# Two products of the feed-forward layers in one 512-column matmul, with the small terms summed apart

## The chip, the cores and the metric

The kernel runs on one core of a Trainium2 chip. The metric is the device time of one execution in microseconds (us), the median of the runs; lower is better. Engines are named as the profile names them: PE is the matmul engine, PEld its weight loads, ACT the scalar engine, DVE the vector engine, POOL the third elementwise engine, SP the engine that issues the weight transfers. Each engine works through its own instructions in the order in which they are written, and they signal each other with semaphores.

## The reference

Four layers at 256 tokens and width 1024, one batch, all in 32-bit floats: stick-breaking attention, retention, gated linear attention and a sparse attention, each followed by a feed-forward layer. The parts that the change touches, cut to their core:

```
def squared_relu_mlp(h, w_up, w_down):      # layers 1 and 2, hidden width 4096
    u = jax.nn.relu(h @ w_up)
    return (u * u) @ w_down

def conv_ffn(h, w_up, conv_w, conv_b, w_down):   # layers 3 and 4, hidden width 2816
    u = h @ w_up                                  # 2 x 2816 columns
    up = jnp.pad(u, ((0, 0), (CONV_WIDTH - 1, 0), (0, 0)))
    u = conv_b + up[:, 0:S] * conv_w[0]
    for j in range(1, CONV_WIDTH):                # CONV_WIDTH = 3
        u = u + up[:, j:j + S] * conv_w[j]
    gate, val = jnp.split(u, 2, axis=-1)
    return (jax.nn.silu(gate) * val) @ w_down

def rmsnorm(x, g):
    y = x * lax.rsqrt(jnp.mean(x * x, axis=-1, keepdims=True) + EPS)
    return y * g
```

## The kernel before, in words

**Products.** Every operand of a large product is split into a high part, rounded to the matmul's `fp32r` type, and a low part, the rest (`w_hi`, `w_lo`, `x_hi`, `x_lo`, `y_hi`, `y_lo`). A product is three matmuls into one PSUM region: high times high, high times low, low times high (`mm3`, lines 562 to 564).

**Weights.** They come in 212 pieces of 128 x 2048 floats, in the order of use. SP loads half pieces into `ring`, which holds four halves; half `q` may be loaded when DVE is done with half `q` - 4 (`stream`, line 373). ACT rounds a half into `w_hi` (line 1222), DVE subtracts and writes `w_lo` (line 1689). `w_hi` and `w_lo` hold four pieces: `refill(g)` loads piece `g` + 4 when PE is done with piece `g`. PE waits for `w_lo` in `split`.

**A feed-forward layer** is `hidden` on PE, and `mlp` (layers 1 and 2) or `ffn` (layers 3 and 4) on ACT and DVE. An up unit `u` is one weight piece, 256 hidden columns in two groups `j` of 128 and eight steps `k` over the width: 48 matmuls of 256 columns that fill one PSUM bank (`transposed`, or `first_unit` for unit 0). MLP layers have 16 up units, conv layers 22. The elementwise engines turn a unit into `y_hi` and `y_lo`. A down piece multiplies them into the accumulators in banks 0 to 3 (`accumulate`, 24 matmuls of 512 columns, `close` for the last ones). In an MLP layer each two up units are followed by two down pieces, one pair of units late. In a conv layer (`ffn`) eight up units come first, then one down piece after each two up units, three pairs late; the last two down pieces are done in `close`, behind all others. Units use six banks in turn (0 and 1 for the first two, then 4 to 7), and unit `u` from 6 on waits until unit `u` - 4 is read out (`freed`).

**The elementwise work of a conv unit**, in the order of each engine:

- DVE: read the bank and multiply by the tokens' scale (`scaled`, line 1736); product of the unit before (1827); `w_lo` of the piece that fell due one step earlier (`refill_behind`, 1689 twice); `y_lo` of the unit before (1833); the two taps of the convolution (1850 twice, 1855 twice).
- ACT: base of the convolution (1308 twice), `y_hi` of the unit before (1302), `w_hi` of the next piece (1222 twice), then silu (1315), which waits for the taps.

An MLP unit has relu (1276) and square into `y_hi` (1279) on ACT, the square (1792) and `y_lo` (1796) on DVE, and one refill on each.

**The tokens' scale.** The norm's factor is applied behind the matmul. POOL computes it from the sum of squares, `spread` on PE turns it into a row (line 553), ACT copies that out of PSUM. In a conv layer PE does `spread` between unit 0 and unit 1.

**The start.** `sb_first` makes the first two pieces in eight quarters; `turn_over` transposes the input in four parts, which ACT and DVE turn into `x_hi` and `x_lo`; `x_tiles` waits for them. `sb_z_` is the attention's first score product and waits for the scaled queries and keys (`sb_unit` on DVE).

## Time and profile before

| | before |
|---|---|
| median of 3 runs | 1383.16 us (1382.28 to 1383.33) |
| the profiled execution's own time | 1384.69 us |
| its span, first to last instruction | 1383.0 us |
| instructions in it | 23122 |
| PE busy | 1345.8 us, 97% |
| DVE busy | 907.9 us, 66% |
| ACT busy | 724.5 us, 52% |
| mean granted PE clock | 0.994 |

The span and the median measure the same thing to 0.2 us; the profiled execution took 1.7 us around its span. Matmuls overlap each other, so a matmul's duration is longer than the distance to the next one; times of a stream of matmuls are read from the distance of their starts.

### The profile page before, as it was taken

How to read it: one execution, taken by the hardware profiler on the slowest of the kernel's cores; microseconds unless marked ns; L12 is line 12 of the kernel's file. 1: busy time of each engine (PE TensorE's matmuls, PEld its weight loads, DVE VectorE, ACT ScalarE, POOL GpSimd, SP SyncE). 2: the span in 40 equal slices, each digit the busy share in tenths (PEclk: the TensorE clock that was granted, in tenths of full speed). 3: DMA queues.
4: the chain of work that ended last, by engine and by line, in shares of the span. 5: the costliest groups of instructions: out<-in, count | busy, mean ns of one | idle time of the engine just before them, and what ended most of it. 6: DMA issues, size and time to landing. Idle time of an engine off the chain costs nothing.

```text
span 1383.0 us, 23122 instructions
## 1 busy us (share of the span) xinstructions
PE 1345.8 (97%) x8826; PEld 1206.3 (87%) x8826; DVE 907.9 (66%) x1417; ACT 724.5 (52%) x1155; POOL 119.2 (9%) x123
## 2 busy tenths in 40 slices
PE   8999999999999999999999999999999988999998
PEld 7887999989987889999888789999888866899997
DVE  4756655557645656555568558777768755697775
ACT  5555544445334545444464446555577535565553
POOL 0001000002500000000002300000002332000000
PEclk9999999999999999999999999999999999999999
DMA  6535655555553446565543345555654310355551
GB/s 229 181 126 196 227 179 201 181 187 172 193 184 126 164 154 227 180 200 183 184 168 125 120 154 183 183 183 187 200 192 153 123 62 32 121 190 187 187 191 70
DMA packets 63887, 231.09 MB, mean 167 GB/s; under 512 B 7088, under 2 KB 7344, under 8 KB 63792
## 3 DMA queue, kind: packets, MB, share of 16 engines
q1 hardware_dynamic: 62208, 224.42, 48.7%
q10 hardware_dynamic: 1584, 5.31, 1.1%
q8 instruction: 70, 1.15, 0.3%
q14 instruction: 25, 0.20, 0.1%
HBM read 228.66 MB, written 1.05 MB: 166 GB/s over the span
## 4 chain that ended last, share of the span: by engine, by line
PE 88%; DVE 5%; ACT 3%; issue 2%; DMA 1%; POOL 0%; POOLq 0%; SPq 0%; DVEq 0%; ACTq 0%
PE ps L562 27%; PE ps L563 26%; PE ps L564 26%; DVE w_lo L1689 2%; DMA ring<-ws 1%; ACT w_hi L1222 1%; DVE x_lo L1709 1%; PE ps L932 1%; ACT x_hi L1242 1%; PE ps L534 1%; PE ps L1124 1%; PE ps L1104 1%; PE ps L856 0%; ACT arena L1217 0%; DVE arena L2242 0%
## 5 line engine op out<-in xcount | busy, mean ns | idle before, releaser
L1689 DVE TENSOR_TENSOR w_lo<-ring,w_hi 128x1024 fp32r<-128x1024 f32 x424 | 513.3, 1250 | 174.4 <-ACT w_hi L1222 173.9
L1222 ACT ACTIVATE w_hi<-ring 128x1024 fp32r<-128x1024 f32 x424 | 429.2, 1052 | 238.9 <-PE ps L564 189.2
L562 PE MATMUL ps<-x_hi,w_hi 128*128 128x256 f32 x1600 | 455.0, 284 | 0.5 <-DVE x_lo L1709 0.5
L563 PE MATMUL ps<-x_lo,w_hi 128*128 128x256 f32 x1600 | 452.7, 283 | 0.0
L564 PE MATMUL ps<-x_hi,w_lo 128*128 128x256 f32 x1600 | 452.6, 283 | 0.0
L562 PEld LDWEIGHTS ps<-x_hi,w_hi 128*128 128x128 f32 x1600 | 306.7, 192 | 4.0 <-issue 3.0
L563 PEld LDWEIGHTS ps<-x_lo,w_hi 128*128 128x128 f32 x1600 | 306.8, 192 | 1.0
L564 PEld LDWEIGHTS ps<-x_hi,w_lo 128*128 128x128 f32 x1600 | 306.8, 192 | 0.0
L562 PE MATMUL ps<-w_hi,y_hi 128*128 128x512 f32 x560 | 221.0, 395 | 2.3 <-issue 2.3
L563 PE MATMUL ps<-w_lo,y_hi 128*128 128x512 f32 x560 | 219.0, 391 | 0.0
L564 PE MATMUL ps<-w_hi,y_lo 128*128 128x512 f32 x560 | 218.6, 390 | 0.0
L562 PEld LDWEIGHTS ps<-w_hi,y_hi 128*128 128x128 f32 x560 | 105.6, 189 | 23.9 <-issue 3.4
L564 PEld LDWEIGHTS ps<-w_hi,y_lo 128*128 128x128 f32 x560 | 105.6, 189 | 22.5
L562 PE MATMUL ps<-w_hi,x_hi 128*128 128x512 f32 (+1 forms) x304 | 121.2, 399 | 3.9 <-DVE x_lo L1709 1.8
L563 PEld LDWEIGHTS ps<-w_lo,y_hi 128*128 128x128 f32 x560 | 105.8, 189 | 20.1
L564 PE MATMUL ps<-w_hi,x_lo 128*128 128x512 f32 (+1 forms) x304 | 115.4, 380 | 0.0
L563 PE MATMUL ps<-w_lo,x_hi 128*128 128x512 f32 (+1 forms) x304 | 115.0, 378 | 0.0
L1736 DVE SCALAR_TENSOR_TENSOR arena<-ps,arena 128x512 f32<-128x512 f32 x64 | 44.1, 690 | 69.0 <-PE ps L564 68.6
L408 POOL TENSOR_TENSOR stat<-stat,power 128x1 f32<-128x1 f32 x20 | 11.6, 585 | 885.4 <-DVE stat L1684 702.7
L1308 ACT ACTIVATE arena<-arena,sm 128x256 f32<-128x256 f32 x88 | 48.2, 595 | 56.7 <-DVE arena L1736 56.7
L562 PEld LDWEIGHTS ps<-w_hi,x_hi 128*128 128x128 f32 x304 | 57.1, 188 | 19.1 <-issue 4.2
L1242 ACT ACTIVATE x_hi<-ps,sm 128x128 fp32r<-128x128 f32 x128 | 35.5, 377 | 70.8 <-PE ps L534 70.8
(227 smaller groups left out, 1305.4 us busy)
## 6 DMA issues: line engine op xcount, KB each, us to landing
ring<-ws SPq DMA_DIRECT2D x424, 512.0 KB, 4.8
tab<-tables ACTq DMA_DIRECT2D x3, 550.0 KB, 5.4
rowg<-rows ACTq DMA_DIRECT2D x3, 512.0 KB, 6.1
h<-x SPq DMA_DIRECT2D x4, 256.0 KB, 5.9
out<-arena SPq DMA_DIRECT2D x4, 256.0 KB, 2.2
arena<-decay ACTq DMA_DIRECT2D x1, 768.0 KB, 8.7
sm<-small ACTq DMA_DIRECT2D x1, 642.0 KB, 4.3
arena<-narrow ACTq DMA_DIRECT2D x1, 296.0 KB, 3.1
```

The lines of the kernel that those rows point to most:

```text
L534: r = nc.tensor.transpose(ps[:, base + k // 2, t * T + (k % 2) * P:t * T + (k % 2 + 1) * P], h[:, t, k * P:(k + 1) * P], ident)
L562: mm(o, lh, rh, start=start, stop=False, skip_group_check=True)
L563: mm(o, lh, rl, start=False, stop=False, skip_group_check=True)
L564: return mm(o, ll, rh, start=False, stop=stop, skip_group_check=True)
L932: r = mm(o, keys, q, start=True, stop=True, skip_group_check=True)
L1104: r = nc.tensor.transpose(ps[:, 6 + i, j * P:(j + 1) * P], ns_s[it % 3][:, i, j * P:(j + 1) * P], ident)
L1124: r = mm(o, v[:, 0, :], p_[:, t * P:(t + 1) * P], start=False, stop=False, skip_group_check=True)
L1222: A(w_hi[:, q // 2 % RING, c:c + HALF], ring[:, q % RAW, :], ACT.Copy).then_inc(hi_ready, 1)
L1242: r = A(dst[:, k, t * P:(t + 1) * P], ps[:, base + b, t * T + (k % 2) * P:t * T + (k % 2 + 1) * P], ACT.Copy, scale=gain(n, k))
L1308: r = A(conv[:, u % 2, e, :], conv_in[:, u % 2, e, :], ACT.Identity, scale=par(u, 4 + e), bias=par(u, 6 + e))
L1689: V.tensor_tensor(w_lo[:, g % RING, v], ring[:, q % RAW, :], w_hi[:, g % RING, v].bitcast(F32), ALU.subtract).then_inc(lo_ready, 1)
L1736: return V.scalar_tensor_tensor(dst, src.rearrange("p (a t) -> p a t", t=T), by, sc.unsqueeze(1).broadcast_to([P, 2, T]), ALU.mult, ALU.mult)
```

## The change

`x_hi` and `x_lo` become the two halves of one tensor `x_both`, side by side for each step `k`. In the up units of all four feed-forward layers `wide` takes the place of `transposed` and `first_unit`: for each `k` and `j` one matmul of 512 columns multiplies `w_hi` by both parts of x, the high product into columns 0 to 255 of a bank, the low one into columns 256 to 511, and one matmul of 256 columns adds `w_lo` times `x_hi` to the latter. A unit is then 16 matmuls of 512 and 16 of 256 columns and fills two banks (`pair_bank`): 0 and 1, 2 and 3, and then 4 and 5 in turn with 6 and 7. Unit `u` from 4 on waits until unit `u` - 2 is read out.

The two sums are added on the way out. ACT copies the small one of the unit to SBUF, DVE adds the large one from PSUM (now `freed`). In the MLP layers DVE then makes the squared relu in one instruction and ACT copies it into `y_hi`. In the conv layers DVE multiplies by the scale in a second instruction. `spread` of the conv layers moves from behind unit 0 to the middle of unit 1, into bank 6, and the first one of the kernel to the middle of piece 3. The first block's quarters, transposes and the elementwise work beside them are reordered.

```diff
-            def first_unit(g, b, n):
+            def wide(g, b, first=None, mid=None):
...
+                for part, j in [(e, j) for e in range(2) for j in range(2)] if first is not None else [(None, 0), (None, 1)]:
+                    if j == 1 and mid is not None:
+                        mid()
+                    for k in range(KT) if part is None else (lower, upper)[part]:
+                        if j == 0 and k % 4 == 0:
+                            split(g, k // 4)
+                        if j == 0 and first is not None:
+                            x_tiles(first, k)
+                        c = k * 256 + j * P
+                        mm(ps[:, b + j, :], w_hi[:, s, c:c + P], x_both[:, k, :, :], start=k == 0, stop=False,
+                           skip_group_check=True)
+                        r = mm(ps[:, b + j, T:2 * T], w_lo[:, s, c:c + P], x_hi[:, k, :], start=False, stop=k == KT - 1,
+                               skip_group_check=True)
+                    if (part, j) == (0, 0):
+                        turn_over(first, 1, part=upper)
...
                 def up(c):
                     for u in (2 * c, 2 * c + 1):
-                        if u >= 6:
-                            pe.wait_ge(freed, at + u - 3)
-                        if u == 0:
-                            first_unit(st.up(c), bank(u), n)
-                        else:
-                            transposed(st.up(c) + u % 2, bank(u))
-                        if u == 0 and n in SCALE_OF:
-                            spread(n)
+                        if u >= 4:
+                            pe.wait_ge(freed, at + u - 1)
+                        if u == 3 and n in SCALE_OF:
+                            pe.wait_ge(scale_ready, SCALE_OF[n] + 1)
+                        wide(st.up(c) + u % 2, pair_bank(u), first=n if u == 0 else None,
+                             mid=(lambda: spread(n, 6)) if u == 1 and n in SCALE_OF else None)
...
-                for q in range(2):
-                    split(g, q)
-                    quarter(0, q)
+                split(g, 0)
+                quarter(0, 0)
                 turn_over(0, 1, part=lower)
+                split(g, 1)
+                quarter(0, 1)
                 turn_over(0, 0, part=upper)
                 quarter(1, 0)
                 quarter(1, 1).then_inc(done, 1)
+                turn_over(0, 1, part=upper)
                 split(g + 1, 0)
                 quarter(0, 2)
-                turn_over(0, 1, part=upper)
                 quarter(1, 2)
...
             sb_first(G_SB, (0, 1))
-            spread(0, 4)
             transposed(G_SB + 2, 2)
-            transposed(G_SB + 3, 3)
+            transposed(G_SB + 3, 3, mid=lambda: spread(0, 4))
```

ACT in an MLP unit:

```diff
-                            act.wait_ge(ready, u - 1)
-                        A(relu[:, u % 2, :], ps[:, bank(u), :], ACT.Relu).then_inc(freed, 1)
-                        act.wait_ge(freed, u + 1)
+                            act.wait_ge(sq, at + u - 1)
+                        A(relu[:, u % 2, :].rearrange("p (a t) -> p a t", t=T), ps[:, b:b + 2, T:2 * T], ACT.Copy)\
+                            .then_inc(low, 1)
+                        act.wait_ge(sq, at + u + 1)
                         i = st.tiles(c)[2 * (u % 2)]
-                        A(y_hi[:, i:i + 2, :], relu[:, u % 2, :].rearrange("p (a t) -> p a t", t=T), ACT.Square)\
+                        A(y_hi[:, i:i + 2, :], square[:, u % 2, :].rearrange("p (a t) -> p a t", t=T), ACT.Copy)\
                             .then_inc(hh, 1)
```

ACT in a conv unit:

```diff
-                        act.wait_ge(freed, at + u + 1)
+                        act.wait_ge(done, st.up(c) + u % 2 + 1)
+                        if u >= 2:
+                            act.wait_ge(freed, at + u - 1)
+                        b = pair_bank(u)
+                        A(conv_small[:, u % 2, :, :], ps[:, b:b + 2, T:2 * T], ACT.Copy).then_inc(low, 1)
+                        act.wait_ge(scaled_in, at + u + 1)
```

DVE in an MLP unit:

```diff
-                        dve.wait_ge(freed, u + 1)
-                        v = relu[:, u % 2, :]
-                        V.tensor_tensor(square[:, u % 2, :], v, v, ALU.mult).then_inc(sq, 1)
+                        dve.wait_ge(low, at + u + 1)
+                        v, b = relu[:, u % 2, :], pair_bank(u)
+                        o = v.rearrange("p (a t) -> p a t", t=T)
+                        V.tensor_tensor(o, ps[:, b:b + 2, 0:T], o, ALU.add).then_inc(freed, 1)
+                        dve.wait_ge(freed, at + u + 1)
+                        V.scalar_tensor_tensor(square[:, u % 2, :], v, 0.0, v, ALU.max, ALU.mult).then_inc(sq, 1)
```

DVE in a conv unit:

```diff
-                        dve.wait_ge(done, g + 1)
-                        scaled(conv_in[:, u % 2, :, :], ps[:, bank(u), :], scale).then_inc(freed, 1)
+                        dve.wait_ge(low, at + u + 1)
+                        b, v = pair_bank(u), conv_in[:, u % 2, :, :]
+                        V.tensor_tensor(v, ps[:, b:b + 2, 0:T], conv_small[:, u % 2, :, :], ALU.add).then_inc(freed, 1)
+                        dve.wait_ge(freed, at + u + 1)
+                        V.tensor_tensor(v, v, scale.unsqueeze(1).broadcast_to([P, 2, T]), ALU.mult).then_inc(scaled_in, 1)
```

ACT, then DVE, in the first block:

```diff
+            hi(2)
             sumsq(0)
-            hi(2)
...
+            lo(2)
             fold(0)
-            lo(2)
...
             dve.wait_ge(scale_ready, SCALE_OF[0] + 1)
+            sb_unit(0)
             refill(G_SB + 1)
-            sb_unit(0)
+            sb_unit(1)
             refill(G_SB + 2)
-            sb_unit(1)
```

How the instructions stand on ACT in a conv layer, from one silu to the next, before the change (`arena` holds all working tiles, so that silu is `arena<-arena` 128x256; behind each row stand the semaphores that it waits for):

```order
L1315 ACTIVATE arena<-arena 128x256 [waits ffn_conv]
L1308 ACTIVATE arena<-arena,sm 128x256 [waits ffn_freed]
L1308 ACTIVATE arena<-arena,sm 128x256
L1302 ACTIVATE y_hi<-arena 128x256 [waits ffn_product]
L1222 ACTIVATE w_hi<-ring 128x1024 [waits weights_in2,piece_done]
L1222 ACTIVATE w_hi<-ring 128x1024 [waits weights_in3]
L1315 ACTIVATE arena<-arena 128x256 [waits ffn_conv]
```

The same place with the change:

```order
L1331 ACTIVATE arena<-arena 128x256 [waits ffn_conv]
L1321 ACTIVATE arena<-ps 128x512 [waits ffn_freed,piece_done]
L1324 ACTIVATE arena<-arena,sm 128x256 [waits ffn_scaled]
L1324 ACTIVATE arena<-arena,sm 128x256
L1313 ACTIVATE y_hi<-arena 128x256 [waits ffn_product]
L1231 ACTIVATE w_hi<-ring 128x1024 [waits weights_in0,piece_done]
L1231 ACTIVATE w_hi<-ring 128x1024 [waits weights_in1]
L1331 ACTIVATE arena<-arena 128x256 [waits ffn_conv]
```

The copy of the small sum of a unit (L1321) stands behind the silu of the unit before it.

DVE in a conv layer, one unit before the change, up to the read-out of the next:

```order
L1736 SCALAR_TENSOR_TENSOR arena<-ps,arena 128x512 [waits piece_done]
L1827 TENSOR_TENSOR arena<-arena 128x256 [waits ffn_silu]
L1689 TENSOR_TENSOR w_lo<-ring,w_hi 128x1024 [waits piece_hi] x2
L1833 TENSOR_TENSOR y_lo<-arena,y_hi 128x256 [waits ffn_hi,ffn_product]
L1850 SCALAR_TENSOR_TENSOR arena<-arena,sm 128x255 [waits ffn_base,ffn_freed]
L1850 SCALAR_TENSOR_TENSOR arena<-arena,sm 128x255
L1855 SCALAR_TENSOR_TENSOR arena<-arena,sm 128x254 [waits ffn_tap]
L1855 SCALAR_TENSOR_TENSOR arena<-arena,sm 128x254
L1736 SCALAR_TENSOR_TENSOR arena<-ps,arena 128x512 [waits piece_done]
```

And with the change:

```order
L1861 TENSOR_TENSOR arena<-ps,arena 128x512 [waits ffn_small]
L1863 TENSOR_TENSOR arena<-arena 128x512 [waits ffn_freed]
L1847 TENSOR_TENSOR arena<-arena 128x256 [waits ffn_silu]
L1705 TENSOR_TENSOR w_lo<-ring,w_hi 128x1024 [waits piece_hi] x2
L1853 TENSOR_TENSOR y_lo<-arena,y_hi 128x256 [waits ffn_hi,ffn_product]
L1873 SCALAR_TENSOR_TENSOR arena<-arena,sm 128x255 [waits ffn_base,ffn_scaled]
L1873 SCALAR_TENSOR_TENSOR arena<-arena,sm 128x255
L1878 SCALAR_TENSOR_TENSOR arena<-arena,sm 128x254 [waits ffn_tap]
L1878 SCALAR_TENSOR_TENSOR arena<-arena,sm 128x254
L1861 TENSOR_TENSOR arena<-ps,arena 128x512 [waits ffn_small]
```

One instruction for the read-out has become two, and the first of them no longer waits for PE's `piece_done` but for ACT's copy (`ffn_small`).

## Rows read from the trace of the kernel before

**Rows 1.** The page: the chain that ended last, by engine.
```profile
PE 88%; DVE 5%; ACT 3%; issue 2%; DMA 1%; POOL 0%; POOLq 0%; SPq 0%; DVEq 0%; ACTq 0%
```

**Rows 2.** Windows of a conv layer: stretch, length, busy time of each engine, clock, DMA.
```profile
860.00:1000.00 140.00, 140.00 (x966) 130.97 (x965) 107.74 (x169) 78.64 (x116) 0.00 (x0) 1.00 0.56 188
```

**Rows 3.** Timeline of PE, end of a conv layer: start, duration, what.
```profile
1002.03 0.39 PE L564 MATMUL ps<-w_hi,y_lo 128*128 128x512 f32 x1
...
1004.07 0.39 PE L564 MATMUL ps<-w_hi,y_lo 128*128 128x512 f32 x1
1004.30 1.03 PE L534 MATMUL ps<-sm,h 128*128 128x128 f32 x8
```

**Rows 4.** Timeline of DVE, start of the first conv layer.
```profile
829.52 0.68 DVE L1736 SCALAR_TENSOR_TENSOR arena<-ps,arena 128x512 f32<-128x512 f32 x1
...
839.13 0.69 DVE L1736 SCALAR_TENSOR_TENSOR arena<-ps,arena 128x512 f32<-128x512 f32 x1 [0.43 <-PE ps L564]
839.74 0.42 DVE L1827 TENSOR_TENSOR arena<-arena 128x256 f32<-128x256 f32 x1
840.07 2.35 DVE L1689 TENSOR_TENSOR w_lo<-ring,w_hi 128x1024 fp32r<-128x1024 f32 x2
842.34 0.42 DVE L1833 TENSOR_TENSOR y_lo<-arena,y_hi 128x256 fp32r<-128x256 f32 x1
842.67 0.87 DVE L1850 SCALAR_TENSOR_TENSOR arena<-arena,sm 128x255 f32<-128x255 f32 x2
843.58 0.88 DVE L1855 SCALAR_TENSOR_TENSOR arena<-arena,sm 128x254 f32<-128x254 f32 x2
844.89 0.69 DVE L1736 SCALAR_TENSOR_TENSOR arena<-ps,arena 128x512 f32<-128x512 f32 x1 [0.43 <-PE ps L564]
```

**Rows 5.** Timeline of ACT beside it.
```profile
840.86 0.40 ACT L1302 ACTIVATE y_hi<-arena 128x256 fp32r<-128x256 f32 x1
841.16 1.99 ACT L1222 ACTIVATE w_hi<-ring 128x1024 fp32r<-128x1024 f32 x2
844.49 0.42 ACT L1315 ACTIVATE arena<-arena 128x256 f32<-128x256 f32 x1 [1.34 <-DVE arena L1855]
```

**Rows 6.** Groups of ACT by form: busy us, mean ns, idle before.
```profile
L1276 ACT ACTIVATE arena<-ps 128x512 f32<-128x512 f32 x32 | 19.1, 597 | 83.2 <-PE ps L564 83.2
```

**Rows 7.** Timeline of DVE around a down piece.
```profile
902.83 2.36 DVE L1689 TENSOR_TENSOR w_lo<-ring,w_hi 128x1024 fp32r<-128x1024 f32 x2
```

**Rows 8.** Timeline of ACT around the same down piece.
```profile
907.96 1.06 ACT L1222 ACTIVATE w_hi<-ring 128x1024 fp32r<-128x1024 f32 x1 [0.29 <-DMA ring<-ws]
910.35 1.06 ACT L1222 ACTIVATE w_hi<-ring 128x1024 fp32r<-128x1024 f32 x1 [1.33 <-DMA ring<-ws]
```

**Rows 9.** The page: DMA issues, KB each, median us from issue to landing.
```profile
ring<-ws SPq DMA_DIRECT2D x424, 512.0 KB, 4.8
```

**Rows 10.** Timeline of DVE, end of the first conv layer.
```profile
993.58 0.42 DVE L1833 TENSOR_TENSOR y_lo<-arena,y_hi 128x256 fp32r<-128x256 f32 x1 [0.56 <-ACT y_hi L1302]
...
1003.13 1.29 DVE L1763 TENSOR_TENSOR h<-ps,h 128x512 f32<-128x512 f32 x2
```

**Rows 11.** Waits: total us, times, longest us.
```profile
PE ps L553 <- POOL stat L408: 2.9, 2, 1.5
```

**Rows 12.** Timeline of PE in the third mixer, behind a wait.
```profile
793.12 0.47 PE L562 MATMUL ps<-w_hi,y_hi 128*128 128x512 f32 x1 [2.34 <-issue]
```

**Rows 13.** Windows around it.
```profile
788.00:800.00 12.00, 9.66 (x40) 7.71 (x39) 7.16 (x10) 4.62 (x7) 2.50 (x2) 0.86 0.53 174
```

**Rows 14.** Timeline of PE, first block and first score product.
```profile
13.92 0.50 PE L562 MATMUL ps<-w_hi,x_hi 128*128 128x512 f32 x1 [0.71 <-DVE x_lo L1709]
...
20.29 0.50 PE L562 MATMUL ps<-w_hi,x_hi 128*128 128x512 f32 x1 [1.14 <-DVE x_lo L1709]
...
39.77 0.28 PE L564 MATMUL ps<-x_hi,w_lo 128*128 128x256 f32 x1
41.23 0.50 PE L758 MATMUL ps<-arena 64*128 64x128 f32 x4 [1.18 <-DVE arena L1736]
```

49 lines of the change are left out of this document (22 added, 27 removed).

## The prediction

> **What bounds the kernel now.** I read the chain that ended last first. It is 88% PE [rows 1]; in a conv layer PE is busy in every one of 140 us, while DVE works in 107.7 and ACT in 78.6 of them [rows 2]. By these averages any saving of matmul time counts, and DVE has a quarter of its time to spare. The average misleads, though: within a conv layer there are stretches of up units alone, and there the timeline of DVE shows only 0.43 us of idle time in a unit of 5.76 us (839.13 to 844.89) [rows 4]. That is the number on which this prediction turns. The reader should see a loop over two engines [rows 4, 5]: DVE reads out a unit, makes the product of the unit before, two halves of `w_lo`, `y_lo` and the taps; ACT's silu waits for the taps (844.49, 1.34 idle [rows 5]).
>
> **Matmuls.** A unit is now 48 matmuls of 256 columns in 5.76 us, 0.120 us each [rows 4]. Nine intervals of 512-column matmuls take 1004.07 - 1002.03 = 2.04 us, 0.227 each [rows 3]. So three small ones, 0.360, become 0.227 + 0.120 = 0.347, and a unit takes 16 x 0.347 = 5.55 us: 0.21 less. The mixed sequence is not in the trace. It could cost nothing beyond its parts, or at worst lose the 0.013 us again and save nothing; I take the parts, since the engine already passes from one width to the other at every down piece. The Trainium skill, "TensorE: Matmul & The Clock Gate", section "Back-to-back issue gap", gives 2.5 ns beyond the columns for a matmul alone; the rows show some 13 ns for both widths [rows 3, 4]. By the skill's figure a unit would save 0.04 us instead of 0.21, and the two MLP layers 1.3 instead of the 6.8 below; the measurement decides.
>
> **MLP layers.** 32 units x 0.21 = 6.8 us less, if the elementwise work keeps up. DVE's loop is add 0.72 (0.69 and 0.03 to the next instruction that needs it), squared relu 0.72, wait for ACT's copy 0.60 + 0.03 [rows 6], `y_lo` 0.61, `w_lo` 2.27 and some 0.4 until its `w_hi` is there: 5.3 us, under 5.55. ACT's next copy doesn't wait for anything late on DVE, and after each two units come two down pieces, 2 x 24 x 0.227 = 10.9 us, with refills alone. The four units at the start could lose a few tenths; I take none. Banks: unit u needs what u - 2 left, a whole unit of 5.55 us ago, and the read-out takes 1.4 us. **-6.8 us** (0 to -6.8).
>
> **Conv layers, unit by unit.** The new order puts ACT's copy of the small sum behind the silu of the unit before, and DVE's add behind that copy. From one add to the next [rows 4 to 6]: add to multiply 0.72; multiply to product 0.61; product to `w_lo` 0.33; two halves 2.27; `y_lo` 0.33; first taps to second 0.91; second taps 0.88; silu starts 0.03 later and lets the next ACT instruction start 0.33 after its own start (as the 0.30 behind `y_hi`); copy 0.60; 0.03 to DVE. Sum 7.04 us, of which the new copy, its place behind silu, and the second pass are 1.71. PE offers a unit each 5.55 us, so it isn't PE that sets the pace any more but this loop. The bank pairs allow PE two units ahead; from unit 5 on it waits for `freed`, 7.04 - 5.55 = 1.5 us each time.
>
> The Trainium skill, "PSUM — Partial Sum Buffer", section "Engine vs sequencer instructions", calls the ScalarE and VectorE queues strict FIFO. If ACT could take the copy ahead of silu, the loop would be only the 6.05 us up to the end of the taps; by the rule it is 7.04. No row of before shows the case, since nothing that stood behind a silu was ready ahead of it.
>
> **Conv layers, with a down piece.** Behind every second unit ACT also fills `w_hi` for the piece of the down step, and stands in front of the next copy until its second half has landed. SP can issue that half only when DVE has made `w_lo` of the second half it replaces. That `w_hi` starts 910.35 - 902.83 = 7.52 us behind DVE's start on the pair, having waited 1.33 for the transfer [rows 7, 8]. The pair starts 0.72 + 0.61 + 0.33 = 1.66 behind the add, so the half starts at 9.18; 0.94 later (1.99 less 1.05, rows 5) the copy, 0.63 later the next add: 10.75. By the median landing of 4.8 [rows 9] from 1.66 + 2.36 it is 4.02 + 4.8 + 0.03 + 0.94 + 0.63 = 10.4. I take 10.6. A pair of units and its down piece then take 7.04 + 10.6 = 17.6 us against PE's 2 x 5.55 + 5.44 = 16.55 (now 16.96). The loop binds here too.
>
> **Sum of a conv layer.** DVE's first read-out is at 829.52 [rows 4] behind `w_lo` work that doesn't change. To the next one 5.35 (no product or refill yet: 0.72 + 0.69 + ACT's base 1.1 + 0.91 + 0.88 and the 1.0 of silu and copy), six loops 42.2, seven pairs 7 x 17.64 = 123.5: the last add is at 1000.6. Its `y_lo` is ready 6.05 + silu 0.45 + product 0.45 + `y_hi` 0.43 + 0.45 = 7.83 later, and only then does `close` start, at 1008.4. Now it starts 30 matmuls ahead of the transposes: 1004.30 - 6.8 = 997.5 [rows 3]. **+10.9 us** in each of the two layers, all savings of matmuls and waits inside it already swallowed.
>
> Behind the first conv layer there is more. From `y_lo` at 994.0 to the residual at 1003.13 DVE needs 9.1 us of refills [rows 10], paced by transfers. Starting at 1008.4 it reaches the residual at 1017.5 and has both halves at 1018.7; PE comes to its transposes at 1008.4 + 6.8 = 1015.2. **+3.5 us.** The last layer has no such refills.
>
> **Clock.** PE's wait ahead of `close` becomes long: unit 21 ends with its two down pieces about 6 us before. After an idle 2.34 us [rows 12] the granted clock over 12 us was 0.86 of 2.4 GHz, the rest at the 1.2 GHz level [rows 13]: 0.14 x 12 = 1.7 us lost. In the first conv layer that hides in the wait for the residual; in the last it counts: **+1.7** (0 to +4). Waits of 1.5 us, as after the spread [rows 11], are not expected to cost it.
>
> **Spread of the scale.** PE now idles 1.46 us at each of the two [rows 11]. Moving it half a unit back removes this, but the first read-out is at 829.52 either way: nothing.
>
> **First block.** PE waits 0.71 and 1.14 us for `x_lo` [rows 14]; each transpose now stands one quarter (6 x 0.227 = 1.4 us) earlier, which covers both, with 0.15 each to refill the pipe. `sumsq` behind `hi(2)` and the spread within piece 3 cost nothing, since a full piece of 5.76 us covers them; the statistics come 2 us later and so does `sb_v`, with two pieces in between. `sb_unit(1)` no longer stands behind a refill, so the 1.18 at the score product [rows 14] goes. Sum 0.71 + 1.14 + 1.18 + 0.15 x 3 = 3.5, a half more for later transfers that start earlier: **-4.0** (-2 to -4.5).
>
> **Sum.** -6.8 - 4.0 + 2 x 10.9 + 3.5 + 1.7 = +16.2. The profiled execution had a span of 1383.0 and 1.7 around it; its span becomes 1399.2. The median of the runs, 1383.16, is the 1.5 us lower of the two totals and becomes 1399.4; I say 1399.5.
>
> **Rivals.**
>
> - *The loop holds, but the transfer is not waited for* (ends on the other side). If the second half landed 1.7 us sooner, the copy would follow at 6.05 + 0.36 + 1.88 + 0.63 = 8.9 and a pair take 15.96, less than PE's 16.55. PE then catches up in the pairs what it lost in the six loops, and `close` starts as now: 1383.2 - 6.8 - 4.0 = 1372. It decides at 10.6 - 16.2 / 14 = 9.4 us for the step with a down piece. For it: landing times scatter. Against: the same transfer behind the same pair of `w_lo` already makes ACT wait 1.33 us [rows 8], with less work on its way. 12%.
> - *The elementwise work never binds*: all 76 units save 0.21 (16.0), the two spreads 2 x 1.6, the start 4.0: 1360. For it: DVE's busy share of 77% [rows 2]. Against: 0.43 us of slack [rows 4], and 1.71 added. 5%.
> - *As forecast, but transfers land later in the new rhythm*, 0.7 us each of 14: 1409. 4%.
> - *A matmul costs 2.5 ns beyond its columns*, so that the MLP layers gain 1.3: 1405. The skill's figure named above; the intervals speak against it [rows 3, 4]. 2%.
> - *The changes cancel*: within 0.2% of now, if the step with a down piece is near 9.4. 3%.
>
> The forecast has the remaining 74%. Its own range is 1391 to 1407: ends of the MLP term (7 us up), of the start (2 up), 10.4 and 10.75 in the step with a down piece (3 down, 2 up), the clock (2 down, 2 up), and half of the tail. 0.2% is 2.8 us, about what a measurement of this kernel can tell from no change. Faster 12 + 5 = 17%, same 3%, slower 80%. The range for 8 in 10 is 1388 to 1408.
>
> **What the profile will show.** Right: the 512-column matmul on x starts 0.120 behind the small one, and that one 0.227 behind it; in MLP layers no idle PE; in conv layers PE idle about 1.5 us ahead of units 5 to 7 for DVE's add, 0.5 to 1 ahead of every odd unit later for `w_lo`, and about 6 us ahead of `close` for `y_lo`; adds 7.0 us apart, 10.6 with a down piece. Wrong: adds 5.55 us apart in the first eight units, which would mean that ACT's copy doesn't wait for silu; no DMA wait of ACT behind odd units; a clock below 1 in the up units. The forecast breaks most easily at the 10.6.

## The result, and the profile with the change

| | before, same chip | with the change |
|---|---|---|
| median of 4 runs | 1382.89 us | 1407.96 us (1403.55 to 1411.57) |
| profiled execution: own time, span | | 1403.55 us, 1401.8 us |
| instructions | | 20860 |
| mean granted PE clock | | 0.991 |

The ratio is 1.018, 95% interval 1.0149 to 1.0211: 25 us slower. The spans of the two profiled executions differ by 1401.8 - 1383.0 = 18.8 us. The profiled execution is the fastest of the four; what follows explains its 18.8 us, and the spread of the others is taken up at the end.

The chain that ended last, by engine, answers [rows 1]:

```profile
PE 63%; DVE 19%; DMA 6%; issue 5%; ACT 5%; POOL 1%; SPq 0%; DVEq 0%; POOLq 0%; ACTq 0%
```

PE has lost a quarter of the chain, and transfers have 6% of it. Busy shares hardly show this: over the same 140 us as in [rows 2], DVE is busy in 113.2 instead of 107.7 us, ACT in 82.9 instead of 78.6, and PE in 130.9 instead of all 140. The second row is the stretch around `close`:

```profile
860.00:1000.00 140.00, 130.90 (x674) 109.97 (x672) 113.22 (x178) 82.90 (x128) 0.00 (x0) 0.99 0.54 177
996.00:1008.00 12.00, 7.10 (x24) 5.76 (x25) 9.01 (x13) 5.65 (x7) 0.00 (x0) 0.72 0.59 180
```

DVE in the ramp, as the first eight up units of a conv layer are called from here on, answering [rows 4]:

```profile
840.95 0.69 DVE L1861 TENSOR_TENSOR arena<-ps,arena 128x512 f32<-128x512 f32 x1 [0.97 <-ACT arena L1321]
841.67 0.69 DVE L1863 TENSOR_TENSOR arena<-arena 128x512 f32<-128x512 f32 x1
842.28 0.42 DVE L1847 TENSOR_TENSOR arena<-arena 128x256 f32<-128x256 f32 x1
842.62 2.35 DVE L1705 TENSOR_TENSOR w_lo<-ring,w_hi 128x1024 fp32r<-128x1024 f32 x2
844.89 0.42 DVE L1853 TENSOR_TENSOR y_lo<-arena,y_hi 128x256 fp32r<-128x256 f32 x1
845.22 0.87 DVE L1873 SCALAR_TENSOR_TENSOR arena<-arena,sm 128x255 f32<-128x255 f32 x2
846.13 0.88 DVE L1878 SCALAR_TENSOR_TENSOR arena<-arena,sm 128x254 f32<-128x254 f32 x2
847.98 0.69 DVE L1861 TENSOR_TENSOR arena<-ps,arena 128x512 f32<-128x512 f32 x1 [0.97 <-ACT arena L1321]
```

and ACT beside it:

```profile
843.71 1.99 ACT L1231 ACTIVATE w_hi<-ring 128x1024 fp32r<-128x1024 f32 x2
847.04 0.42 ACT L1331 ACTIVATE arena<-arena 128x256 f32<-128x256 f32 x1 [1.34 <-DVE arena L1878]
847.36 0.58 ACT L1321 ACTIVATE arena<-ps 128x512 f32<-128x512 f32 x1
```

Two engines wait for each other in a ring: DVE's add waits 0.97 us for ACT's copy, the copy stands behind silu, and silu has waited 1.34 us for DVE's taps. One round is 847.98 - 840.95 = 7.03 us.

ACT where a down piece comes in:

```profile
892.28 0.42 ACT L1331 ACTIVATE arena<-arena 128x256 f32<-128x256 f32 x1 [1.34 <-DVE arena L1878]
893.26 1.06 ACT L1231 ACTIVATE w_hi<-ring 128x1024 fp32r<-128x1024 f32 x1 [0.56 <-DMA ring<-ws]
895.89 1.06 ACT L1231 ACTIVATE w_hi<-ring 128x1024 fp32r<-128x1024 f32 x1 [1.57 <-DMA ring<-ws]
896.86 0.58 ACT L1321 ACTIVATE arena<-ps 128x512 f32<-128x512 f32 x1
```

and DVE's adds ahead of it and behind it:

```profile
886.18 0.69 DVE L1861 TENSOR_TENSOR arena<-ps,arena 128x512 f32<-128x512 f32 x1 [0.97 <-ACT arena L1321]
...
897.47 0.69 DVE L1861 TENSOR_TENSOR arena<-ps,arena 128x512 f32<-128x512 f32 x1 [2.96 <-ACT arena L1321]
```

The copy, which needs nothing but PE's sum, stands behind two transfers, and the add follows 11.29 us after the last one. PE pays in four places (timeline of PE, one row for each kind of wait): for the bank that DVE's add frees, for `w_lo`, ahead of `close`, and at the transposes behind it:

```profile
848.72 0.50 PE L603 MATMUL ps<-x_both,w_hi 128*128 128x512 f32 x1 [1.11 <-DVE arena L1861]
...
907.53 0.47 PE L603 MATMUL ps<-x_both,w_hi 128*128 128x512 f32 x1 [1.24 <-DVE w_lo L1705]
...
1000.90 0.80 PE L569 MATMUL ps<-w_hi,y_hi 128*128 128x512 f32 x1 [6.24 <-DVE y_lo L1853]
1011.54 1.25 PE L541 MATMUL ps<-sm,h 128*128 128x128 f32 x8 [2.02 <-DVE h L1779]
```

In the MLP layers PE has no such waits; the edge of a down piece and a unit shows both widths:

```profile
228.82 0.39 PE L571 MATMUL ps<-w_hi,y_lo 128*128 128x512 f32 x1
229.05 0.39 PE L603 MATMUL ps<-x_both,w_hi 128*128 128x512 f32 x1
...
230.10 0.40 PE L603 MATMUL ps<-x_both,w_hi 128*128 128x512 f32 x1
230.34 0.28 PE L605 MATMUL ps<-x_both,w_lo 128*128 128x256 f32 x1
230.45 0.40 PE L603 MATMUL ps<-x_both,w_hi 128*128 128x512 f32 x1
```

A good way to place a difference is to cut the span at marks that every version has. Here they are PE's first transposes of each norm, which begin the start, the layers and the mixers in turn (us; each entry is the distance of two marks read from PE's timeline; the last two columns are explained below):

| stretch | before | change | difference | `copy_ahead_all` | `copy_ahead_of_refill` |
|---|---|---|---|---|---|
| start and first mixer | 129.1 | 124.7 | -4.4 | 125.9 | 125.6 |
| MLP layer 1 | 179.7 | 177.9 | -1.8 | 178.2 | 177.9 |
| second mixer | 198.5 | 198.4 | -0.1 | 198.5 | 198.4 |
| MLP layer 2 | 181.5 | 179.7 | -1.8 | 179.7 | 180.1 |
| third mixer | 124.7 | 124.7 | 0.0 | 124.7 | 123.1 |
| conv layer 1 | 190.8 | 206.1 | +15.3 | 189.0 | 194.4 |
| fourth mixer | 177.4 | 175.4 | -2.0 | 176.0 | 176.2 |
| conv layer 2 to the end | 201.3 | 214.9 | +13.6 | 197.4 | 203.3 |
| span | 1383.0 | 1401.8 | +18.8 | 1369.4 | 1379.0 |

### The profile page after: what moved, and what is told of

The parts are those of the page before. It is cut to its first block, busy times and chain, and to the rows that moved or that the text cites. A ratio compares the mean times of both kernels' runs of the same rounds, so it can differ in the third digit from the quotient of the medians.

```text
span 1401.8 us, 20860 instructions
## 1 busy us (share of the span) xinstructions
PE 1342.4 (96%) x7610; PEld 1141.0 (81%) x7610; DVE 961.3 (69%) x1493; ACT 746.8 (53%) x1199; POOL 120.1 (9%) x123
## 4 chain that ended last, share of the span: by engine, by line
PE 63%; DVE 19%; DMA 6%; issue 5%; ACT 5%; POOL 1%; SPq 0%; DVEq 0%; POOLq 0%; ACTq 0%
PE ps L569 14%; PE ps L571 13%; PE ps L570 13%; PE ps L603 10%; DVE w_lo L1705 7%; DMA ring<-ws 6%; PE ps L605 5%; DVE arena L1861 2%; DVE arena L1863 2%; DVE arena L1878 2%; ACT arena L1321 2%; DVE arena L1873 2%; ACT w_hi L1231 1%; DVE arena L1847 1%; PE ps L941 1%
## 5 line engine op out<-in xcount | busy, mean ns | idle before, releaser
L603 PE MATMUL ps<-x_both,w_hi 128*128 128x512 f32 x1216 | 432.7, 399 | 15.0 <-DVE arena L1861 8.2
L605 PE MATMUL ps<-x_both,w_lo 128*128 128x256 f32 x1216 | 340.6, 280 | 0.0
L603 PEld LDWEIGHTS ps<-x_both,w_hi 128*128 128x128 f32 x1216 | 228.3, 188 | 76.5 <-issue 11.0
L605 PEld LDWEIGHTS ps<-x_both,w_lo 128*128 128x128 f32 x1216 | 229.5, 189 | 0.9
L569 PE MATMUL ps<-w_hi,x_both 128*128 128x512 f32 (+1 forms) x304 | 121.9, 401 | 1.7 <-DVE x_both L2285 0.9
L571 PE MATMUL ps<-w_hi,x_both 128*128 128x512 f32 (+1 forms) x304 | 116.1, 382 | 0.0
L570 PE MATMUL ps<-w_lo,x_both 128*128 128x512 f32 (+1 forms) x304 | 115.8, 381 | 0.0
L569 PE MATMUL ps<-x_both,w_hi 128*128 128x256 f32 x384 | 110.1, 287 | 0.0
L570 PE MATMUL ps<-x_both,w_hi 128*128 128x256 f32 x384 | 108.6, 283 | 0.0
L571 PE MATMUL ps<-x_both,w_lo 128*128 128x256 f32 x384 | 108.6, 283 | 0.0
L415 POOL TENSOR_TENSOR stat<-stat,power 128x1 f32<-128x1 f32 x20 | 11.6, 586 | 909.3 <-DVE stat L1700 712.9
L569 PEld LDWEIGHTS ps<-x_both,w_hi 128*128 128x128 f32 x384 | 73.5, 191 | 1.4 <-issue 1.3
L570 PEld LDWEIGHTS ps<-x_both,w_hi 128*128 128x128 f32 x384 | 73.6, 192 | 0.0
```

Source lines behind the costliest of these rows:

```text
L569: mm(o, lh, rh, start=start, stop=False, skip_group_check=True)
L570: mm(o, lh, rl, start=False, stop=False, skip_group_check=True)
L571: return mm(o, ll, rh, start=False, stop=stop, skip_group_check=True)
L603: mm(ps[:, b + j, :], w_hi[:, s, c:c + P], x_both[:, k, :, :], start=k == 0, stop=False, skip_group_check=True)
L605: r = mm(ps[:, b + j, T:2 * T], w_lo[:, s, c:c + P], x_hi[:, k, :], start=False, stop=k == KT - 1, skip_group_check=True)
```

## The experiments

The theory was the prediction's: the ring of ACT's copy, silu and the taps, and the transfers ahead of the copy. Its rival was that the change costs time elsewhere too, in the matmuls or by new transfers. All kernels are versions of the changed one, except where the text says that it is one of the kernel before. Ratios are to the kernel before on the same chip, where its median was 1384.4 to 1386.5 us; each is given with its 95% interval. The expectations went by the 1382.9 us of the first chip. A time "brought to it" below is the ratio times 1382.9, and it is the one to hold against an expected time.

### ACT's copy moved ahead of silu

`small(u)` is the wait and copy of the small sum of unit `u`, which in the change begins a unit. `copy_ahead_part` moves it ahead of silu, but not past the refill of a down piece:

```diff
-                        act.wait_ge(done, st.up(c) + u % 2 + 1)
...
-                        A(conv_small[:, u % 2, :, :], ps[:, b:b + 2, T:2 * T], ACT.Copy).then_inc(low, 1)
+                        if u == 0:
+                            small(0)
...
                         refill(st.up(c) + u % 2)
+                        if u % 2 == 0 or c < st.ahead:
+                            small(u + 1)
                         act.wait_ge(conv_done, at + u + 1)
...
                         refill(st.down(c))
+                    if c + st.ahead + 1 < st.chunks:
+                        small(2 * (c + st.ahead + 1))
```

> ACT copies the small sum of conv unit u+1 before the silu of unit u, wherever no down piece stands between them; the work itself and the bank pairs stay as changed. Theory (the loop over two engines sets the pace, because the copy stands behind silu): DVE's adds come 5.96 us apart in the first eight units instead of 7.03 (taps 0.79 to the next add instead of 1.86), a step with a down piece stays near 10.6, a pair takes about 16.7 and is bound by PE; PE waits for DVE fall to about 0.3 us a unit, the wait ahead of the last down pieces shrinks from 6 us to about 1, and the total is 1364 to 1372 us. Rival (what costs is the added DVE and ACT work, or two bank pairs instead of six banks, in whatever order): the total stays within 4 us of the changed kernel's 1408.

Measured: 1380.9 us, ratio 0.9963 (0.9947 to 0.9979). Adds are 5.97 us apart in the ramp, and 10.0 to 11.3 us with a down piece, much as without the edit. Brought to the first chip that is 1377.8 us, 6 above the expected range. A pair with its down piece still takes 10.8 + 5.97, about 16.8 us, no less than PE's own 16.8, so DVE never catches up with PE, and PE waits 2.07 and 2.97 us ahead of the two `close`.

`copy_ahead_all` also puts the copy between silu and the down piece's refill:

```diff
                     if u == units - 1:
                         product_hi(u)
+                    elif c >= st.ahead:
+                        small(u + 1)
```

> As the run with the copy ahead of silu, but the copy also stands ahead of the refill that follows a down piece, so that it doesn't wait for that refill's transfer. Theory: steps with a down piece fall to PE's pace (about 11.1 us with the pair's other step at 5.6), PE never waits for w_lo in the conv layers, no long wait ahead of the last down pieces; 1362 to 1368 us, at or some us below the partial version. Rival (added work or bank pairs): still above 1395 us. If transfers do not matter at all, it equals the partial version within 1 us.

Measured: 1370.73 us, ratio 0.9898 (0.9881 to 0.9914), 1% faster than before. DVE's adds in the ramp:

```profile
840.11 0.68 DVE L1869 TENSOR_TENSOR arena<-ps,arena 128x512 f32<-128x512 f32 x1
...
846.08 0.68 DVE L1869 TENSOR_TENSOR arena<-ps,arena 128x512 f32<-128x512 f32 x1
```

and ACT between them:

```profile
842.86 1.99 ACT L1231 ACTIVATE w_hi<-ring 128x1024 fp32r<-128x1024 f32 x2
844.76 0.58 ACT L1320 ACTIVATE arena<-ps 128x512 f32<-128x512 f32 x1
846.19 0.42 ACT L1337 ACTIVATE arena<-arena 128x256 f32<-128x256 f32 x1 [0.86 <-DVE arena L1886]
```

The copy now lies in the time in which ACT waited for the taps, and the add no longer waits. Steps with a down piece are 8.25 us, until the adds settle at 10.82 and 5.98 in turn, which is PE's own pair of 16.8. Everything the change lost in the conv layers comes from the place of one instruction. Brought to the first chip the time is 1368.8 us, 1 us above the expected range; the matmul pair gains less than was thought, as comes up below.

`copy_ahead_of_refill` makes the second move without the first: behind silu, but ahead of the down piece's refill.

```diff
+                        if u == 0 or u % 2 == 1 or c <= st.ahead:
+                            small(u)
...
                     if u == units - 1:
                         product_hi(u)
+                    elif c >= st.ahead:
+                        small(u + 1)
```

> The changed kernel with one edit: where a down piece makes VectorE and ScalarE do more in a step, ScalarE's copy of the next even unit stands behind silu as in the change, but ahead of the refill's split instead of behind it. In the first units of a convolution layer, which have no down piece, nothing is moved. Theory (the add waits for the copy, and the copy stands behind whatever ScalarE does after the gate): adds stay 7.03 us apart without a down piece; a step with one falls from 10.6 us to about 8.2 (5.97 of the short step plus 2.3 of the split), so that a pair of units takes about 15.3 us, less than the 16.7 that TensorE needs for its matmuls, and TensorE sets the pace again behind the ramp: 1371 to 1377 us. Rival (the 7.03 us loop of the first units costs most of it): above 1395 us.

Measured: 1382.2 us, ratio 0.9977 (0.9966 to 0.9988). The first step with a down piece, 868.75 to 877.00, and the step behind it:

```profile
868.75 0.69 DVE L1867 TENSOR_TENSOR arena<-ps,arena 128x512 f32<-128x512 f32 x1 [0.97 <-ACT arena L1320]
...
877.00 0.68 DVE L1867 TENSOR_TENSOR arena<-ps,arena 128x512 f32<-128x512 f32 x1
...
884.41 0.69 DVE L1867 TENSOR_TENSOR arena<-ps,arena 128x512 f32<-128x512 f32 x1 [1.36 <-ACT arena L1320]
```

Steps are 7.03 in the ramp and 8.25 with a down piece, as expected, and at the end 9.76 and 7.03 in turn at PE's pace; but brought to the first chip the total is 1379.7 us, 3 above the range. I had left out that the ramp's loss is not won back: the two conv layers take 5.4 and 5.9 us more than with both moves (table). So the place behind the refill costs 11.7 + 11.6 us of the change's loss, and the place behind silu the other 5.4 + 5.9. The moves don't add up in the other order (`copy_ahead_part` alone gains 13.0 + 14.1): whichever is made first gains most, since PE's pace limits both together.

### Half of each transfer left out

To tell the transfers from ACT's own work, each weight transfer behind the first four halves carries only half its columns; the rest of the weights in SBUF stays old, so that part of the product is made from other data. It is done to both kernels:

```diff
-                sp.dma_start(ring[:, q % RAW, :], src).then_inc(weights_in[q % RAW], 16)
+                n = HALF if turn is None and q < RAW else HALF // 2
+                sp.dma_start(ring[:, q % RAW, 0:n], src[:, 0:n]).then_inc(weights_in[q % RAW], 16)
```

> The changed kernel with each half weight piece transferred only half (512 of its 1024 columns; the other columns keep what the first four halves brought), so that a transfer lands sooner and the output is not the reference's. All instructions of the engines stay. Theory (the step with a down piece waits for the transfer of the refill, then the copy): adds without a down piece stay 7.03 us apart, steps with one fall from 10.6 us on average to about 9.2, PE regains in the pairs what it lost; 1388 to 1396 us. Rival (transfers are hidden, the work alone sets the pace): equal to the changed kernel's 1404 to 1411 us.

> The same halved transfers in the kernel before, as a control. Theory: PE is the bound there and transfers are hidden but for the start and some mixers; at most 3 us less than 1382.9. If halving the transfers made every kernel faster by more, the run of the changed kernel would tell nothing of its loop.

Measured: 1380.26 us for the change (0.9958, 0.9944 to 0.9972) and 1382.09 us for the kernel before (0.9972, 0.9961 to 0.9984). ACT at a down piece:

```profile
908.65 0.42 ACT L1332 ACTIVATE arena<-arena 128x256 f32<-128x256 f32 x1 [1.34 <-DVE arena L1879]
908.97 2.24 ACT L1232 ACTIVATE w_hi<-ring 128x1024 fp32r<-128x1024 f32 x2
911.11 0.58 ACT L1322 ACTIVATE arena<-ps 128x512 f32<-128x512 f32 x1
```

The split no longer waits, and the step falls from 10.6 to 9.2 us on the mean of both layers; the ramp keeps its 7.03. I had expected the changed kernel at least 11 us above this (1377.1 us, brought to the first chip). With a pair of 16.2, under PE's 16.8, DVE catches up with PE by half a microsecond in each pair, and the long waits ahead of `close` go (6.24 to 1.15 us in the first layer, 6.26 to nothing of note in the second). The two conv layers take 194.6 and 203.4 us, 11.5 less each than in the changed kernel. Seven steps with 1.4 us less waiting for transfers make 9.8 of each 11.5. In the control nothing of this is seen: its four feed-forward layers take 179.7, 181.6, 190.8 and 201.3 us, the kernel before's own times to 0.1. Its total fell by 3.9 us by the ratio, 0.9 more than the expected most; in the profiles the start gives 2.1 us and the third mixer 1.6.

### The feed-forward layers 3 and 4 as before

`conv_as_before` keeps the change in the MLP layers and at the start, and gives the conv layers their old matmuls, read-out and place of `spread`:

```diff
+                        if n in SCALE_OF:
...
+                            if u == 0:
+                                first_unit(st.up(c), bank(u), n)
+                            else:
+                                transposed(st.up(c) + u % 2, bank(u))
+                            if u == 0:
+                                spread(n)
+                            continue
```

`conv_as_before_spread` has `spread` in the middle of unit 1 instead.

> The MLP layers and the first block as changed; the two conv layers and their spread of the scale as before. Theory: all of the loss is in the conv layers, so this is faster than before: start 4.3 us and MLP layers 1.85 us each as the changed kernel's profile shows, 1374 to 1375 us; up to 2 us less if the third stretch of gain, in the sparse attention, is a matter of the layout and not of when it starts. Rival (part of the loss comes from the MLP layers' extra work, from the layout x_both or from transfers in general): above 1379 us.

> As the run with the conv layers as before, but their spread of the scale stands in the middle of unit 1. Theory: PE no longer idles 1.46 us at each of the two spreads and the pipe isn't refilled there, 1.6 us each: 3.2 us less than with the spread behind unit 0, so 1371 to 1372 us. Rival (DVE's first read-out is late either way, so nothing is gained): equal within 0.5 us.

Measured: 1376.65 us (0.9945, 0.9923 to 0.9967) and 1374.42 us (0.9918, 0.9901 to 0.9934); brought to the first chip 1375.3 and 1371.6, within 0.3 us of what was expected. The parts of the change outside the conv layers gain: 7.6 us by the first ratio, 9.3 by the spans.

The profile of the first has the two waits of 1.47 us at `spread` that [rows 11] show, the second has none of them. The medians differ by 2.2 us and their intervals overlap; the spans, 1373.7 and 1372.6, differ by 1.1. The marks of the table tell more. The conv layers take 191.3 and 201.3 us in the first and 189.8 and 199.6 in the second, 3.2 less together, as expected. The three traces with the old matmuls and the old place of `spread` (`before`, `half_transfers_before`, `conv_as_before`) have no less than 190.8 and 201.3, and `grouped_matmuls`, built on the second, has 189.2 and 199.6. What hides it in the spans is the clock in the third mixer: 123.0 us at a granted clock of 1.00 in the first, 124.6 at 0.99 in the second. Both have the same wait of PE of 2.3 us there, after which the clock fell in one execution and not in the other. All fourteen traces are of one kind or the other, 123.0 or 123.1 us in four and 124.6 or 124.7 in ten.

### The start as before

`start_as_before` is `copy_ahead_all` with the first block in its old order:

```diff
-                split(g, 0)
-                quarter(0, 0)
+                for q in range(2):
+                    split(g, q)
+                    quarter(0, q)
                 turn_over(0, 1, part=lower)
-                split(g, 1)
-                quarter(0, 1)
...
+            spread(0, 4)
             transposed(G_SB + 2, 2)
-            transposed(G_SB + 3, 3, mid=lambda: spread(0, 4))
+            transposed(G_SB + 3, 3)
...
```

> The kernel with the copy ahead everywhere, and the first block's order of quarters, transposes, halves, spread and scaled units as in the kernel before. Theory (the new order removes waits of 0.71, 1.14 and 1.18 us and the pipe's refill behind them): 4.0 to 4.4 us slower than with the new order. Rival (the gain of the start is given back later, at the waits for transfers and attention weights in the first mixer): equal within 1 us.

Measured: 1374.83 us (0.9924, 0.9909 to 0.994), against 1370.73 with the new order. PE's waits are back as in [rows 14]:

```profile
13.53 0.50 PE L569 MATMUL ps<-w_hi,x_both 128*128 128x512 f32 x1 [0.70 <-DVE x_both L1733]
19.88 0.50 PE L569 MATMUL ps<-w_hi,x_both 128*128 128x512 f32 x1 [1.14 <-DVE x_both L1733]
21.95 0.50 PE L569 MATMUL ps<-w_hi,x_both 128*128 128x512 f32 x1 [0.40 <-DVE w_lo L1713]
41.26 0.50 PE L767 MATMUL ps<-arena 64*128 64x128 f32 x4 [1.63 <-DVE arena L1760]
```

The first stretch of the table becomes 128.9 us, 3.0 more than `copy_ahead_all`'s, and no later stretch gives back more than 0.4 of it; the spans differ by 2.4 us and the medians by 4.1. So the gain of the start is real, 2.4 to 4.1 us by these figures, where 4.0 to 4.4 were expected.

### Why the matmul pair gains little

Over a whole layer the 512-column matmul of an up unit is followed after 235 ns (median over the kernel; 233 to 236 in single layers), where one of a down piece is followed after 227; the small one after 117 ns instead of 120. The pair takes 0.352 us and not 0.347, and a unit 5.63 us. Four kernels look for the reason. `grouped_matmuls` (on `conv_as_before_spread`) and `copy_ahead_grouped` (on `copy_ahead_all`) put four of one width behind each other:

```diff
+                        for k in ks:
+                            c = k * 256 + j * P
+                            r = mm(ps[:, b + j, T:2 * T], w_lo[:, s, c:c + P], x_hi[:, k, :], start=False,
+                                   stop=k == KT - 1, skip_group_check=True)
```

> The kernel with conv layers as before and the spread in unit 1, in which the MLP layers' up units issue four matmuls of 512 columns and then four of 256 instead of taking turns. Theory (a matmul of 256 columns between two of 512 costs some 5 ns a pair more than its two kinds cost in streams of their own: 235 + 117 against 227 + 120): pair 0.347, each MLP layer 16 x 16 x 5 ns = 1.3 us shorter, 2.6 in all. Rival (the extra is that of a matmul on x_both in two banks or of the pair's addresses, whatever the order): equal within 0.5 us.

> The copy ahead everywhere, with the matmuls grouped by four in the up units of all feed-forward layers. If grouping saves 5 ns a pair as supposed, 76 units x 16 x 5 ns = 6 us less than with the copy ahead alone, as far as DVE's 5.96 us a unit in the first eight conv units allows; if the order of the widths is indifferent, the same within 1 us.

Measured: 1374.46 us (0.9908, 0.9888 to 0.9929) and 1367.7 us (0.9866, 0.9849 to 0.9882). The order is not indifferent, but grouping by four gives less than half of what was hoped. Over all up units in which PE neither waited nor had the low clock, the mean pair is 0.350 us in both grouped kernels and 0.352 or 0.353 in every other one. The MLP layers take 177.4 and 179.2 to 179.3 us, where all ten other traces with the new matmuls have 177.8 to 178.2 and 179.7 to 180.1; in `copy_ahead_grouped` the four feed-forward layers together take 2.6 us less than in `copy_ahead_all`. The ratios go the same way (0.9866 against 0.9898, intervals that just touch). The two spans, 1369.1 and 1369.4 us, don't show it, because the profiled execution of `copy_ahead_grouped` was the slowest of its four, at a granted clock of 0.991 where the others had 0.995 or 0.996: its fourth mixer took 2.4 us more.

`flat_pattern` (on `copy_ahead_all`) gives the streamed operand as one run of 512 columns instead of two of 256:

```diff
-x_both[:, k, :, :], start=k == 0, stop=False,
+x_both[:, k, :, :].rearrange("p a t -> p (a t)"), start=k == 0, stop=False,
```

> The kernel with the copy ahead everywhere, in which the 512-column matmul reads x_both through a flat pattern of 512 elements instead of 2 x 256 (the same bytes in the same order). Theory (the two-level read pattern costs the 7 ns by which this matmul's distance of 234 exceeds the 227 of the down pieces' matmuls): the pair falls from 0.352 to 0.346, unit 5.53, each MLP layer 1.5 us shorter, the total some 4 to 6 us less. Rival (it is something else about this matmul): distances of 233 to 235 again, and the same time within 1 us.

Measured: 1370.72 us (0.9884, 0.9868 to 0.9901), and again 236 and 117 ns. `stream_weights` (on `copy_ahead_all`) streams other data:

```diff
-w_hi[:, s, c:c + P], x_both[:, k, :, :], start=k == 0, stop=False,
+w_hi[:, s, c:c + P], w_hi[:, s, c // 512 * 512:c // 512 * 512 + 512], start=k == 0, stop=False,
```

> The kernel of copy_ahead_all with one operand changed: in the up units of all four feed-forward layers the 512-column matmul streams 512 columns of w_hi instead of the two parts of x; its stationary operand, its place between the small matmuls and its bank stay. The computation is changed by this: the hidden units are products of weights with weights. Behind the 512-column matmul the next one starts 234 to 236 ns later with x_both streamed, and 227 ns in the down pieces, where w_hi and w_lo are streamed. Theory (what is streamed, or where it lies, makes the 8 ns): the distance becomes 227 ns, the pair 0.344 us, and the kernel 76 x 16 x 8 ns = 9.7 us faster at most, 1361 to 1367 us. Rival (the bank, the place beside a matmul into half of the same bank, or the weight half kept still): the distance stays 233 to 236 ns and the time 1369 to 1373 us.

Measured: 1370.17 us (0.9902, 0.9886 to 0.9919):

```profile
229.96 0.39 PE L603 MATMUL ps<-w_hi 128*128 128x512 f32 x1
230.19 0.28 PE L605 MATMUL ps<-x_both,w_lo 128*128 128x256 f32 x1
230.30 0.40 PE L603 MATMUL ps<-w_hi 128*128 128x512 f32 x1
```

The median is still 235 ns, and in both runs the time stayed where the rival had it. Neither the pattern nor what is streamed makes the 8 ns.

The traces themselves say more than these kernels, if one asks at which place in the sequence a large matmul is slow. With the four and four of `copy_ahead_grouped`, the first group of a unit that follows a down piece stands behind large matmuls only:

```profile
229.81 0.39 PE L571 MATMUL ps<-w_hi,y_lo 128*128 128x512 f32 x1
230.04 1.07 PE L605 MATMUL ps<-x_both,w_hi 128*128 128x512 f32 x4
230.94 0.64 PE L609 MATMUL ps<-x_both,w_lo 128*128 128x256 f32 x4
231.42 1.09 PE L605 MATMUL ps<-x_both,w_hi 128*128 128x512 f32 x4
232.35 0.63 PE L609 MATMUL ps<-x_both,w_lo 128*128 128x256 f32 x4
```

Its four are followed after 227 ns each (0.90 us in all). The next four have operands of the same kind and add to the same bank, and take 0.93. The other way round, the large matmuls of a down piece are slow while small ones stand a few places ahead of them. In the kernel before, the first five behind a unit are followed after 233, 236, 228, 232 and 231 ns (1.16 us), the next five after 227 (1.14):

```profile
223.79 0.40 PE L562 MATMUL ps<-w_hi,y_hi 128*128 128x512 f32 x1
...
224.95 0.39 PE L564 MATMUL ps<-w_hi,y_lo 128*128 128x512 f32 x1
```

In the changed kernel it is the first ten of a down piece, with means from 226 to 237 ns, and 227 from the eleventh on. So what goes with the 8 ns is neither what is kept still nor the bank, but small matmuls among the last few ahead of a large one, and a group of four is too short to leave them behind. Why a small matmul has this effect, and whether groups of sixteen would be rid of it, no run shows.

## Why the prediction was right

**The ring of two engines.** Forecast 7.04 us from add to add, measured 7.03. That the copy stands behind silu costs what was worked out: moved ahead of it, adds are 5.97 us apart. The Trainium skill, "PSUM — Partial Sum Buffer", section "Engine vs sequencer instructions", calls the ScalarE and VectorE queues strict FIFO; these runs agree, since in the rows above a copy whose sum had been complete for almost 7 us began only 847.36 - 847.04 = 0.32 us behind the start of silu. The signs came as named: PE waited 1.1 to 1.35 us for DVE's add ahead of units 5 to 7 in the first conv layer and 4 to 7 in the second. Only the waits for `w_lo` ahead of odd units were fewer, seven above 0.5 us where fourteen were expected.

**The step with a down piece.** Forecast 10.6 us, measured 10.66 in the first conv layer and 10.49 in the second (means of seven, 9.79 to 11.29). ACT's wait for the second half was 1.57 us in the rows above against the 1.33 assumed. This was called the weakest number; half of the transfer's bytes takes it to 9.2. The first distance of all, from unit 0 to unit 1, was forecast at 5.35 us (its terms add up to 5.30) and was 5.41 in the first layer, but 6.70 in the second.

**The conv layers.** Forecast +10.9 each, +3.5 behind the first, +1.7 for the clock in the last: +14.4 and +12.6. Measured +15.3 and +13.6. `close` was to start 1008.4 - 829.52 = 178.9 us behind the first read-out and started 1000.90 - 821.5 = 179.4 behind it. Counted like this the two layers lost 11.5 us each up to `close`, against the 10.9. PE idled 6.24 and 6.26 us there, and the granted clock was 0.72 of 2.4 GHz over the 12 us around either wait. What that costs can be read from the distances of the matmuls in the last layer:

```profile
1382.62 0.79 PE L569 MATMUL ps<-w_hi,y_hi 128*128 128x512 f32 x1 [6.26 <-DVE y_lo L1853]
...
1385.35 0.63 PE L569 MATMUL ps<-w_hi,y_hi 128*128 128x512 f32 x1
1385.78 0.63 PE L570 MATMUL ps<-w_lo,y_hi 128*128 128x512 f32 x1
...
1388.63 0.39 PE L569 MATMUL ps<-w_hi,y_hi 128*128 128x512 f32 x1
```

At the 1.2 GHz level they follow each other after 427 ns. The 18 distances from 1382.62 to 1388.63 take 6.01 us instead of 18 x 0.227 = 4.09: 1.9 us lost, forecast 1.7. In the first conv layer PE lost 1.7 us in the same way and then still waited 2.02 us for the residual, so there it cost nothing, as forecast.

**The start.** Forecast -4.0, measured -4.4 (-3.2 in `copy_ahead_all`). The waits of 0.71, 1.14 and 1.18 us of [rows 14] are gone; what is left is 0.60 and 0.19 for `w_lo`:

```profile
19.10 0.50 PE L569 MATMUL ps<-w_hi,x_both 128*128 128x512 f32 x1 [0.19 <-DVE w_lo L1705]
```

**The MLP layers.** This term was mis-sized: forecast -6.8, measured -1.8 - 1.8 = -3.6. The mechanism was right, with no idle PE, but the pair was 0.352 and not 0.347 us: 16 x 0.008 = 0.13 us per unit instead of 0.21, and 32 x 0.13 = 4.1. The two prices of the parts were read in sequences where each had its own neighbours. The prediction took the mixing as free because PE already passes from one width to the other at every down piece; it had not read what that pass costs, and the rows of 223.79 to 224.95 above, from the kernel before, had the answer. (Its product, 32 x 0.21, is 6.7 and not 6.8; that changes nothing.) The Trainium skill, "TensorE: Matmul & The Clock Gate", section "Back-to-back issue gap", gives 2.5 ns beyond the columns for a matmul alone. An estimate by it was a gain of 1.3 us; the measured distances are 235 - 213 = 22 and 117 - 107 = 10 ns beyond the columns, and the layers lie between the two forecasts. In the conv layers the same error shortens nothing, since the ring sets the pace.

**Spread.** Forecast 0 with the ring. Its wait is gone, and DVE's first read-out still comes 16.1 us behind the first transpose in the first conv layer, before and with the change. Where PE sets the pace it is worth 1.5 and 1.7 us, as `conv_as_before_spread` shows.

**The fourth mixer** was to stay and took 2.0 us less. The eleven traces of the other versions of the change, none of which edits it, have 175.8 to 179.3 us there, in step with the granted clock: 0.97 or 0.98 where it took up to 176.5 us, 0.95 or 0.96 in the four with 177.7 or more. The clock was 0.97 in the kernel before and 0.98 with the change, and a hundredth of 177 us is 1.8 us, so most of this gain can be the clock's chance. About 1 us may be real: at 0.97 the versions of the change take 175.8 to 176.2 us, and the two traces of the kernel before (one with halved transfers) 177.4 and 176.9.

**The sum.** Forecast +16.2 for the span, measured +18.8: 3.2 too little gained in the MLP layers, 1.9 more lost in the conv layers, 2.5 gained at the start and in the mixers. These errors go both ways and in part cancel, and the gain in the mixers is largely chance. The forecast of 1399.5 us stands against 1403.55 for the profiled execution and 1407.96 for the median. The median lies above the forecast's own range (up to 1407) and within the wider one (up to 1408) by 0.04 us, so the number itself was right by luck; what was right by reasoning is the mechanism and the size of its parts. The other three runs take 3 to 8 us longer than the profiled one, while the runs before lie within 1.1 us. That fits a path with some 14 transfers on it, whose landing times scatter, but those runs have no trace, and it stays an argument.

**The rivals.** *Transfer not awaited*, 1372 us, was almost made real by the halved transfers, and they gave 1377.1, brought to the first chip. The rival's price was wrong: it let PE win back in seven pairs what it had lost in the ramp. A shorter pair lets DVE catch up with PE, but PE's own 16.8 us a pair don't shrink, so its waits in the ramp stay lost. Each costs 7.03 - 5.63 = 1.4 us, three times in the first layer and four times in the second, which is 4.2 (and 1.15 ahead of `close`) and 5.6 us. The layers took 5.6 and 5.9 us more than in `copy_ahead_all`. *Never binds*, 1360 us, is bounded by `copy_ahead_all`: 1368.8, brought to the first chip, the 9 us more being mostly the 76 units at 0.13 instead of 0.21 us (6) and the wait of 2.12 us for the residual.

## What to carry to other kernels

In a loop over two in-order engines, what counts is not the work of each but the longest way round: an instruction that is ready early, and on which the other engine waits, belongs ahead of whatever waits in its own queue. Here one 0.58 us copy behind a silu and behind two transfers turned a saving of 1% into a loss of 1.8%. An engine that is 77% busy on average can have 0.43 us to spare in the rounds that matter, so read the slack there. And read the price of a mixed sequence of matmuls at a place of the trace where the two widths meet: adding the distances that each has among its own kind forecast almost twice the gain that came.
